# Prompt attention of a hybrid streaming encoder: the order of scores and probability transposes on TensorE

## What is computed

```python
def _attend(q, k, v, pos_q, pos_k, frame_causal, cum_q=None, cum_k=None):
    scale = q.shape[-1] ** -0.5
    logits = jnp.einsum('bqhd,bkhd->bhqk', q, k).astype(jnp.float32) * scale
    if cum_q is not None:
        logits = logits + cum_q[..., :, None] - cum_k[..., None, :]
    ...
    p = jax.nn.softmax(jnp.where(mask, logits, NEG_INF), axis=-1)
    return jnp.einsum('bhqk,bkhd->bqhd', p.astype(v.dtype), v)
```

## Time and profile before

| | |
|---|---|
| median of 3 runs | 2857.41 us (2855.22 to 2858.92) |
| profiled execution | 2855.53 us |
| its span, first to last instruction | 2853.7 us |
| PE busy | 2737.4 us, 96% of the span |
| DVE busy | 1750.5 us, 61% |
| ACT busy | 1069.6 us, 37% |
| POOL busy | 1037.9 us, 36% |

### The profile page before, as it was taken

The page is one execution under the profiler, slowest core; times in us unless marked ns, Lnnn a source line. Parts: engine busy times, 40 slices in busy tenths (PEclk is TensorE's granted clock), DMA queues, the critical chain, the costliest instruction groups (busy, mean ns, idle before and its releaser), DMA issues.

```text
span 2853.7 us, 39612 instructions
## 1 busy us (share of the span) xinstructions
PE 2737.4 (96%) x14966; PEld 2212.7 (78%) x14966; DVE 1750.5 (61%) x2216; ACT 1069.6 (37%) x1968; POOL 1037.9 (36%) x574
## 2 busy tenths in 40 slices
PE   8998999899999999999999989998999999999997
PEld 6986666787888887888779766667878888878886
DVE  4036776634564559888740367775356554688887
ACT  4225544423333332333332355444243233333333
POOL 1111000014544456767511200000145444567666
PEclk9999999999999999999999999999999999999999
DMA  4211001332333346343132200013323434653441
GB/s 142 63 30 53 18 17 44 134 133 96 122 130 131 147 174 244 132 142 127 64 113 65 56 17 17 17 44 134 137 92 133 152 116 144 240 191 129 138 148 74
DMA packets 164242, 306.91 MB, mean 108 GB/s; under 512 B 24688, under 2 KB 90384, under 8 KB 164112
## 3 DMA queue, kind: packets, MB, share of 16 engines
q1 hardware_dynamic: 160800, 301.75, 30.3%
q10 hardware_dynamic: 3312, 3.41, 0.4%
HBM read 207.40 MB, written 97.72 MB: 107 GB/s over the span
## 4 chain that ended last, share of the span: by engine, by line
PE 84%; DVE 8%; issue 3%; ACT 2%; DMA 1%; POOL 1%; SPq 0%; DVEq 0%; ACTq 0%; POOLq 0%
PE ps L2544 7%; PE ps L2548 7%; PE ps L2546 7%; PE ps L2454 7%; PE ps L2455 7%; PE ps L2456 7%; PE ps L2215 6%; PE ps L2067 5%; PE ps L2065 5%; PE ps L2066 5%; PE ps L2245 4%; PE ps L2268 4%; PE ps L2330 1%; PE ps L2184 1%; PE ps L2399 1%
## 5 line engine op out<-in xcount | busy, mean ns | idle before, releaser
L2544 PE MATMUL ps<-wq_hi,sa_hi 128*128 128x512 f32 x896 | 350.1, 391 | 5.2 <-DVE x L1999 5.2
L2548 PE MATMUL ps<-wq_hi,sa_lo 128*128 128x512 f32 x896 | 349.7, 390 | 0.0
L2546 PE MATMUL ps<-wq_lo,sa_hi 128*128 128x512 f32 x896 | 349.7, 390 | 0.0
L967 POOL TENSOR_TENSOR w_lo<-w_raw,w_hi 128x1024 fp32r<-128x1024 f32 (+2 forms) x32 | 70.2, 2195 | 646.8 <-ACT w_hi L1145 646.8
L1937 DVE TENSOR_TENSOR sa_lo<-ra,sa_hi 128x1024 fp32r<-128x1024 f32 x112 | 284.7, 2544 | 23.4 <-ACT sa_hi L1431 23.4
L1999 DVE TENSOR_TENSOR x<-ps,x 128x1024 f32<-128x1024 f32 x224 | 264.2, 1212 | 56.2 <-PE ps L2548 50.5
L1042 POOL TENSOR_TENSOR wq_lo<-wsum,wq_hi 128x1024 fp32r<-128x1024 f32 x64 | 157.3, 2459 | 291.0 <-ACT wq_hi L1411 291.0
L2065 PE MATMUL ps<-w_hi,hT_hi 128*128 128x512 f32 (+2 forms) x672 | 248.7, 370 | 0.0
L2067 PE MATMUL ps<-w_hi,hT_lo 128*128 128x512 f32 (+2 forms) x672 | 246.3, 366 | 0.0
L2066 PE MATMUL ps<-w_lo,hT_hi 128*128 128x512 f32 (+2 forms) x672 | 245.3, 365 | 0.0
L1929 DVE TENSOR_TENSOR cq<-ps,cq 128x1024 f32<-128x1024 f32 x48 | 58.7, 1222 | 286.3 <-ACT cq L1472 244.2
(11 more groups left out here) (324 smaller groups left out, 6274.6 us busy)
## 6 DMA issues: line engine op xcount, KB each, us to landing
ra<-hidden_scratch SPq DMA_DIRECT2D x112, 512.0 KB, 3.3
hidden_scratch<-cq SPq DMA_DIRECT2D x94, 512.0 KB, 2.7
rq<-in_w_up_dram SPq DMA_DIRECT2D x64, 512.0 KB, 3.9
rq<-in_w_down_dram SPq DMA_DIRECT2D x64, 512.0 KB, 4.3
residual_scratch<-x SPq DMA_DIRECT2D x27, 512.0 KB, 3.1
x<-residual_scratch SPq DMA_DIRECT2D x27, 512.0 KB, 7.6
x<-in_x_prompt_dram SPq DMA_DIRECT2D x16, 512.0 KB, 7.5
w_raw<-in_w_in_dram SPq DMA_DIRECT2D x16, 512.0 KB, 4.3
```

What stands on the lines that cost most here:

```text
L2544: pe.matmul(out, ah[:, k, :], bh[:, k * 512:(k + 1) * 512], start=new and k == 0, stop=False, skip_group_check=True)
L2546: pe.matmul(out, ah[:, k, :], bl[:, k * 512:(k + 1) * 512], start=False, stop=False, skip_group_check=True)
L2548: last = pe.matmul(out, al[:, k, :], bh[:, k * 512:(k + 1) * 512], start=False, stop=final and k == 1, skip_group_check=True)
```

## The change

In each step PE issues the scores of its unit first, and then the transposes of the probabilities of the unit three steps back. V stays behind both. No instruction is added or removed, and the lists of DVE, ACT, POOL and SP are unchanged.

```diff
                 for i in range(len(UNITS) + LAG):
+                    if i < len(UNITS):
+                        scores(i)
                     if i >= LAG_T and i - LAG_T < len(UNITS) and is_attn(i - LAG_T):
                         probs_transposes(i - LAG_T)
-                    if i < len(UNITS):
-                        scores(i)
                     if i == len(UNITS) + 2:
                         wuk_transposes()
```

## The result

| | before | after |
|---|---|---|
| median, runs taken beside each other | 2857.6 us (2854.83 to 2859.39) | 2864.91 us (2863.23 to 2868.75) |
| ratio after / before, 95% interval | | 1.0030 (1.0020 to 1.0041) |
| profiled execution | 2855.53 us | 2868.75 us |
| stage, first S to V of unit 90, layer 0 | 286.78 us | 290.38 us |
| the same, layer 1 | 286.68 us | 290.36 us |

The change costs 7.3 us: 0.26% by the two medians, 0.30% (0.20 to 0.41%) by the ratio of the runs. By the prediction's bound of 0.2% this is slower, if only just. In the profiled executions the two stages together are 3.60 + 3.68 = 7.28 us longer, as much as the medians differ. The profiled executions themselves differ by more, 13.2 us. The other 6 lie outside the stage: in the execution of after five stretches of half clock there are 6.8 us long that are 3.4 us long in the one of before.

The account below looks back on a forecast made before the run. PE, busy 96% of the span, bounds the kernel, so only its gaps can be won. The terms sum to +1.95 us a layer, +3.9 on 2855.5; with 1.9 to the median, 2861 us, 8-in-10 range 2851 to 2869.

Parts of the forecast that it names:

- Part 1, the circle that stays: Tile 4: T, its copy, norm, next T take 2.10 us; T's waits of 0.25 to 0.33 remain, so no gain.
- The walk through tiles 0 to 3: Layer 0's instructions moved with durations kept; new waits make the first T of tile 4 2.85 us late.
- q1 and T(80): Tiles 5 to 7: scores fill T's waits near q1 and at T(80): -0.6, -0.2 and -0.7 us.
- Swa in tiles 4 to 6: Behind swa, S of the third mla unit waits 1.0 to 1.2 for exp; balance +0.1, +0.3, +0.2 us.
- The new circle: S(i), T(i-3), copy, norm, max, exp, S(i+2): 4.91 us against 5.12 in tile 4; 0.8 to spare in tile 7.
- The rival of the new circle in the steady steps: Mla units, tiles 3 to 6: the new circle binds, costing 2.7 us more a layer: 2867 us; chance 0.31.
- The clock's rival: Shorter waits in the stage let neither half-clock stretch happen, 3.2 us back: 2858 us; chance 0.12, inside "no change".
- The faster rival: Scores fill T's waits wherever S could stand, 5 us a layer: 2847 us; chance 0.09; sign: T waits under 4.
- Other engines: POOL's padding and SP's load start 0.5 to 0.9 earlier, nobody waits: 0; at most one copy of tens of ns.

Follow-up runs that it names:

- e5: Kernel before, TensorE order unchanged, with VectorE doing norm ahead of the copies: 2852.40 us, ratio 0.9980.
- e1_early: Kernel before, with the new order (scores first) only in steps 0 to 29, tiles 0 to 3: 2864.74 us, ratio 1.0024.
- e10: Changed kernel with the old order (transposes before scores) put back at steps 6, 11 and 88: 2862.40 us, ratio 1.0021 to the kernel before.
- e2_late: Kernel before, with the new order only from step 30 on, tiles 4 to 7: 2861.05 us, ratio 1.0011.
- e3: Kernel before, with scores first only in 14 chosen steps where T waits while the gate of S is open: 2850.81 us, ratio 0.9977.
- e7: Kernel before, with scores first in 13 chosen steps, the list of e3 without step 24: 2848.01 us, ratio 0.9965.
- e8: Kernel before, with scores first in the 13 steps of e7 and norm ahead of the copies on VectorE: 2844.32 us, ratio 0.9951.
- e4: Changed kernel, with VectorE doing max first, then copies, then norm in attention steps: 2882.80 us, ratio 1.0086 to the kernel before.
- e6: Changed kernel, with VectorE doing norm ahead of the copies: 2845.24 us, ratio 0.9963 to the kernel before.
- e9: Kernel e8 with scores first in two steps more, 7 and 18 (15 steps): 2841.37 us, ratio 0.9943 to the kernel before.

## Why the prediction was right or wrong

The forecast was 2861 us and "no change, on its slow side"; the time is 2864.9, inside the range of 2851 to 2869, outside the forecast's own 2855 to 2863, and by 0.26% on the side that had the chance of 0.31. That it came so near is partly luck. The sum was one of waits, +1.95 us a layer, and waits grew by 1.65 in layer 0. The step that failed is the one under it, that each instruction keeps its duration: PE's own work, put at nothing, became 3.3 us a layer longer. The clock, left out of the sum, then gave back 2.9 over both layers.

- **Part 1, the circle that stays: right.** It takes 2.04 us in tile 4 against 2.10, the exchange won nothing there, and e5 shows that it is this circle: with norm out of it the 0.25 are gone. The sign that was named for it failed, though: the 0.25 does not stand at T(38), it stands at the weights of S(41) ahead of it.
- **The walk through tiles 0 to 3: the places right, 2.85 forecast, 3.17 measured** (3.48 in e1_early), **but made of other parts.** The 2.85 were all waits; measured are 1.89 of waits and 1.27 of longer work on PE. S(6) was to wait 1.8 and waits 1.68, S(11) 0.9 and waits 0.64, V of 13 1.1 and waits 0.99; but S(17), S(18), S(20) and S(27) wait 0.13 to 0.19 where 0.3 to 0.4 were forecast. e1 shows that this lateness is carried to the end unchanged, e10 that 1.1 of it hangs on steps 6 and 11.
- **q1 and T(80): right.** V of 43 -0.46 (forecast -0.6), V of 58 -0.14 (-0.2), T(80) -0.61 in layer 1, where no half clock is in the way (-0.7).
- **Swa in tiles 4 to 6: mis-sized.** The three terms were +0.1, +0.3 and +0.2; measured are +0.49, +0.69 and +0.85. S of the third mla unit waits 0.88, 1.01 and 1.10 for exp, as forecast, and all waits of PE in these stretches together grow by 0.24 us, less than the 0.6 of the sum. The other 1.8 us are PE's own work. They come in steps of 0.04 to 0.25 at nearly every V. In e2_late V of 26 and V of 27, the first two in the new order, are 0.05 and 0.06 later with no wait at all. I had taken S, T and V to be as long in the new order as in the old; the wide S whose weights are not loaded ahead (38 of 54 in after, 2 in before) are 0.1 us longer.
- **S(88): missed.** The new circle was given 0.8 of room in tile 7, with a V in the two steps. Steps 86 and 87 have none. 6.44 us against 5.46 of PE work costs 0.98. The walk allowed for a missing V in tile 3 alone.
- **The rival of the new circle in the steady steps:** it asked for waits at every other mla step, and those are not there: S(41) waits 0.14. Its size came out all the same, by luck: tiles 4 to 7 lost 4.95 - 3.17 = 1.8 us a layer, where my terms gave -0.9 and the rival's 2.7 on top of them 1.8. Where the circle does bind is at S(88) and behind swa.
- **The clock's rival came true** inside the stage: no half clock is left there, and 2.9 us come back, beside 3.2 forecast. The Trainium skill (TensorE: Matmul & The Clock Gate, Part 1: The HAM clock gate) says that an idle PE is throttled and that activity lifts the throttle; the stage's clock of 1.00 agrees, though the runs below show that the length of a wait alone does not decide.
- **The faster rival fell, but its sign did not:** T's waits are at 2.4 us a layer, under the 4 that were to speak for it. Waits of T alone were a poor sign, since the exchange hands them to S.
- **Other engines: 0, right.** No wait of PE in the stage of after ends with POOL or a DMA. A padding copy takes 0.40 us (1.58 us for 4 in the earlier trace rows), though, and not the tens of ns that were named as the risk.

By place the sum was too low by 3.0 us a layer: 0.3 in tiles 0 to 3, 0.1 each at V of 43, V of 58 and T(80), 1.4 in the swa terms, 0.95 at S(88). The clock's 2.9 us for both layers, left out of the sum, took half of it away again: 2861.3 + 6.0 - 2.9 = 2864.4, beside 2864.9 measured.

## What to carry to other kernels

To move ready work behind gated work on an in-order engine is a gain only in the steps where the gate is open, and only if what hangs behind the moved instruction on the other engines does not come late: write down each circle of queues that the moved instruction joins, step by step, and drop from PE's share every instruction that some steps don't have. Then see what the moved instruction stands behind: here busy time grew by 3.3 us a layer for the same instructions, twice as much as the waits, and no view of waits shows that. A wait that changes its owner without becoming shorter points to such a circle; look for the instruction in it that could have run earlier (here norm, which stood behind a copy that it does not need). Of two queues that feed each other the order has to be chosen together: norm first gains 0.2% with the old order on TensorE, and turns the new one from 0.30% slower into 0.37% faster.

## What the runs showed of the hardware

The same wait is followed by full clock or by half clock. The wait of 1.98 before T(4) stands in both layers of before, e2, e3, e5, e7 and e8, twelve times; half clock follows in four (before and e7 in layer 1, e5 in both). The wait of 2.17 before T(80) stands six times in before, e1 and e5, and half clock follows in three. A wait of 2.21 before T(4) in e4 is followed by half clock in both layers. A stretch costs 1.35 to 1.59 us here. In after and e10, whose longest wait in the stage is 1.7, no stretch stands there. But e6 has the same longest wait, and in its layer 0 half clock sets in at V of 90 (517.9 us, clock 0.50 for 3.4 us); the waits just before it are 0.44 at T(89) and 1.09 two us earlier. The same stretch at the stage's end stands in layer 0 of e3, e4, e8 and e9 and in layer 1 of e8. So a wait of 2 us is neither enough for half clock nor needed for it.

PE's busy time is not fixed by its instructions: at a clock of 1.00 the 1,997 matmuls of a stage take 271.9 us in after, 268.3 in e6 and 266.8 in e8. The number of wide S whose first weights are loaded ahead goes the same way: 16, 20 and 44 of 54.
